# One modulation pair of a delta-rule layer, formed with one-column TensorE products beside the S5 stage

## The reference

```python
c_act = jax.nn.silu(c)
for i in range(DEPTH):
    mod = c_act @ ada_w[i] + ada_b[i]
    sh1, sc1, g1, sh2, sc2, g2 = [m[:, None, :] for m in jnp.split(mod, 6, axis=-1)]
    h = x * (1.0 + sc1) + sh1
    ...
    x = layer_norm(ALPHA * x + (1.0 + g1) * y, ln1_g[i], ln1_b[i])
```

## Time and profile before

| | |
|---|---|
| runs | 2766.16, 2773.31, 2775.39 us; median 2773.31 us |
| the profiled execution | 2767.55 us, its span 2765.9 us |
| TensorE matmul | 2542.9 us busy, 92% of the span |
| VectorE | 2046.9 us, 74% |
| ScalarE | 1220.4 us, 44% |
| chain that ended last | TensorE 74%, VectorE 17%, DMA 3% |
| granted TensorE clock, mean | 0.953 of 2.4 GHz |

### The profile page before, as it was taken

The page is one execution under the profiler, slowest core; times in us unless marked ns, Lnnn a source line. Parts: engine busy times, 40 slices in busy tenths (PEclk is TensorE's granted clock), DMA queues, the critical chain, the costliest instruction groups (busy, mean ns, idle before and its releaser), DMA issues.

```text
span 2765.9 us, 41894 instructions
## 1 busy us (share of the span) xinstructions
PE 2542.9 (92%) x16532; PEld 2298.9 (83%) x16532; DVE 2046.9 (74%) x2518; ACT 1220.4 (44%) x1614; POOL 197.5 (7%) x226
## 2 busy tenths in 40 slices
PE   1499998888889999999999899998999999999998
PEld 1488777777878899889988799998878998899887
DVE  8879999778587777777778888568887655555556
ACT  1255555544455433443343453453464434443444
POOL 0012332000000000000001011000000000000000
PEclk8589999888899999999999899999999999999998
DMA  9874444556448788888888499556588665555652
GB/s 374 285 254 143 152 151 149 195 172 203 138 153 302 272 276 275 277 280 278 277 274 291 154 335 337 173 168 219 183 276 280 214 195 186 190 190 184 196 184 77
DMA packets 272987, 616.02 MB, mean 223 GB/s; under 512 B 23211, under 2 KB 23746, under 8 KB 272578
## 3 DMA queue, kind: packets, MB, share of 16 engines
q1 hardware_dynamic: 240020, 488.00, 52.2%
q0 software_dynamic: 32640, 125.84, 13.0%
q10 hardware_dynamic: 174, 0.04, 0.0%
HBM read 611.73 MB, written 2.10 MB: 222 GB/s over the span
## 4 chain that ended last, share of the span: by engine, by line
PE 74%; DVE 17%; issue 3%; DMA 3%; ACT 2%; SPq 2%; DVEq 0%; POOL 0%; POOLq 0%
PE groups L2530 11%; PE groups L2534 11%; PE groups L2532 11%; PE groups L2538 10%; PE groups L2542 10%; PE groups L2540 10%; DMA ada_units<-in_ada_w_dram 3%; DVE ada_acc L2032 2%; DVE w_lo L2050 2%; SPq L1659 1%; PE pc L2709 1%; DVE ada_acc L872 1%; PE pb L2699 1%; DVE ada_acc L2357 1%; PE groups L1131 1%
## 5 line engine op out<-in xcount | busy, mean ns | idle before, releaser
L1749 ACT ACTIVATE w_hi<-w_raw 128x1024 fp32r<-128x1024 f32 x776 | 817.3, 1059 | 1136.1 <-PE groups L2534 544.6
L2050 DVE TENSOR_TENSOR w_lo<-w_raw,w_hi 128x1024 fp32r<-128x1024 f32 x747 | 905.5, 1223 | 530.4 <-ACT w_hi L1749 526.4
L2530 PE MATMUL groups<-w_hi,act_hi 128*128 128x512 f32 x1408 | 553.4, 393 | 19.8 <-DVE act_lo L2184 19.8
L2534 PE MATMUL groups<-w_lo,act_hi 128*128 128x512 f32 x1408 | 549.9, 391 | 0.0
L2532 PE MATMUL groups<-w_hi,act_lo 128*128 128x512 f32 x1408 | 549.9, 391 | 0.0
L2538 PE MATMUL groups<-act_hi,w_hi 128*128 128x256 f32 x1776 | 511.6, 288 | 33.3 <-DVE act_lo L2184 13.9
L2540 PE MATMUL groups<-act_lo,w_hi 128*128 128x256 f32 x1776 | 503.1, 283 | 0.0
L2542 PE MATMUL groups<-act_hi,w_lo 128*128 128x256 f32 x1776 | 503.0, 283 | 0.0
L2538 PE MATMUL groups<-hid_hi,w_hi 128*128 128x256 f32 x1392 | 390.6, 281 | 0.0
L2542 PE MATMUL groups<-hid_hi,w_lo 128*128 128x256 f32 x1392 | 388.9, 279 | 0.0
L2540 PE MATMUL groups<-hid_lo,w_hi 128*128 128x256 f32 x1392 | 388.9, 279 | 0.0
(11 more groups left out here) (440 smaller groups left out, 2498.6 us busy)
## 6 DMA issues: line engine op xcount, KB each, us to landing
ada_units<-in_ada_w_dram POOLq DMA_DIRECT2D x120, 1024.0 KB, 6.5
w_raw<-in_ffn_w_gate_dram SPq DMA_DIRECT2D x88, 1024.0 KB, 5.2
w_raw<-in_ffn_w_up_dram SPq DMA_DIRECT2D x88, 1024.0 KB, 5.3
w_raw<-in_ffn_w_down_dram SPq DMA_DIRECT2D x88, 1024.0 KB, 5.1
w_raw<-in_cd_w_in_dram SPq DMA_DIRECT2D x48, 1024.0 KB, 5.8
w_raw<-in_ab_w_in_dram SPq DMA_DIRECT2D x40, 1024.0 KB, 5.8
ada_units<-in_ada_w_dram SPq DMA_DIRECT2D x80, 512.0 KB, 4.4
w_raw<-in_ab_w_out_dram SPq DMA_DIRECT2D x16, 1024.0 KB, 6.0
```

Of the source, the lines that this page charges most:

```text
L1749: act.activation(whi[:, half, k], raw[:, slot, k], ACT.Copy).then_inc(hi_done, 1)
L2050: dve.tensor_tensor(wlo[:, half, k], raw[:, slot, k], whi[:, half, k].bitcast(F32), ALU.subtract).then_inc(lo_done, 1)
L2530: pe.matmul(dst, hi[:, k, rows], whi[:, j % 2, kk], start=(k == 0), stop=False, skip_group_check=True)
L2534: last = pe.matmul(dst, hi[:, k, rows], wlo[:, j % 2, kk], start=False, stop=(k == UK * p["units"] - 1), skip_group_check=True)
```

## The change

For the first pair, VectorE's sums go away. TensorE takes each loaded slice as weights and the column of `c_act` that belongs to it as the moving operand: eight products of one column (`ada_columns`), which add up in `pm` over the 16 slices. They stand behind the 48 matmuls of the same 16 units, ahead of `s5_out`. The first pair has no `ada_sum` in the GLU product any more. The semaphore `dn_ada_dve` is called `dn_ada_used`, and TensorE raises it for the first 16 slices; SyncE waits for it at the same places. `take(0)` waits for the count 16 of it.

```diff
--- before.py
+++ after.py
@@ -173,7 +173,7 @@
 
 def pe_names():
 
-    names = [f"ada{b}" for b in range(EARLY_PAIRS)] + ["nq0", "nk0", "gi0", "bi0", "gram0"]
+    names = ["nq0", "nk0", "gi0", "bi0", "gram0"]
     for i in range(ROUNDS):
         nxt = i + 1 < ROUNDS
         early = ["", f"gi{i + 1}", f"bi{i + 1}", "", "", f"nq{i + 1}", ""]
@@ -400,7 +400,7 @@
         dne = Marks(sem("dn_pe"), pe_names())
         dnp = Marks(sem("dn_pool"), pool_names())
         dn_ada_in = [sem(f"dn_ada_in{n}") for n in range(4)]
-        dn_ada_dve = sem("dn_ada_dve")
+        dn_ada_used = sem("dn_ada_used")
         level_masks = sem("dn_level_masks")
         scd = Steps(sem("sc_dve"), "m c0 c1 c2 g", start=1)
         mix_hi, mix_lo = sem("mix_hi"), sem("mix_lo")
@@ -567,7 +567,7 @@
             if m == 0:
                 sp.wait_ge(ada_step, 16 * glu["ab1"] + ADA_FREE)
             if m > 3:
-                sp.wait_ge(dn_ada_dve, m - 3)
+                sp.wait_ge(dn_ada_used, m - 3)
             rows, block = P * (m % 16), glu["ab1"] + 2 * (m // 16)
             sp.dma_start(ada_slot(m), ada_w[0][rows:rows + P, GROUP * block:GROUP * block + 2 * GROUP]
                          ).then_inc(dn_ada_in[m % 4], 16)
@@ -864,17 +864,25 @@
             unit, total = ada_slot(n), ada_total(pair)
             dve.wait_ge(dn_ada_in[n % 4], 16 * (n // 4 + 1))
             if k == 0:
-                if pair > 1:
+                if pair > 2:
                     dve.wait_ge(dne.sem, dne.at(f"ada{pair - 2}"))
                 last = dve.tensor_scalar(total, unit, cact[:, 0:1], None, ALU.mult)
             else:
-                dve.wait_ge(dn_ada_dve, n)
+                dve.wait_ge(dn_ada_used, n)
                 last = dve.scalar_tensor_tensor(total, unit, cact[:, k:k + 1], total, ALU.mult, ALU.add)
-            last.then_inc(dn_ada_dve, 1)
+            last.then_inc(dn_ada_used, 1)
+
+        def ada_columns(pe, m):
+
+            if m == 0:
+                pe.wait_ge(mod_taken, glu["ab1"] + 1)
+            pe.wait_ge(dn_ada_in[m % 4], 16 * (m // 4 + 1))
+            for t in range(2 * GT):
+                last = pe.matmul(pm[:, t:t + 1], ada_slot(m)[:, P * t:P * t + P], cact[:, m:m + 1], start=(m == 0 and t == 0),
+                                 stop=(m == KT - 1), skip_group_check=True)
+            last.then_inc(dn_ada_used, 1)
 
         def deltanet_early_dve(dve, n):
-            if n in EARLY_AT:
-                ada_op(dve, EARLY_AT.index(n))
             if n in CONV_AT:
                 convolve(dve, 0, [CONV_AT.index(n)])
             if n == 30:
@@ -1006,7 +1014,10 @@
                                               ALU.mult, ALU.subtract), f"lo{i}")
 
             def take(pair):
-                on(dne, f"ada{pair}")
+                if pair:
+                    on(dne, f"ada{pair}")
+                else:
+                    dve.wait_ge(dn_ada_used, KT)
                 c = GT * (glu["ab1"] + 2 * pair)
                 done(dve.tensor_tensor(mod[:, c:c + 2 * GT], pm[:, 0:2 * GT], adab[:, c:c + 2 * GT], ALU.add), f"take{pair}")
                 if pair == 0:
@@ -1273,19 +1284,14 @@
                 done(last, f"x{i}.{k}")
 
             def ada_sum(pair):
-                if pair:
-                    on(dnd, f"take{pair - 1}")
-                else:
-                    pe.wait_ge(mod_taken, glu["ab1"] + 1)
-                pe.wait_ge(dn_ada_dve, KT * (pair + 1))
+                on(dnd, f"take{pair - 1}")
+                pe.wait_ge(dn_ada_used, KT * (pair + 1))
                 for t in range(2 * GT):
                     last = pe.matmul(pm[:, t:t + 1], ada_total(pair)[:, P * t:P * t + P], ones[:, 0:1], start=True, stop=True)
                 done(last, f"ada{pair}")
 
             for n in range(4):
                 side(glu, n)
-            for pair in range(EARLY_PAIRS):
-                ada_sum(pair)
             side(glu, 4)
             norm_q(0)
             norm_k(0)
@@ -2711,6 +2717,8 @@
 
             def s5_after(i, j):
                 n = 8 * i + j
+                if n in EARLY_AT:
+                    ada_columns(pe, EARLY_AT.index(n))
                 s5_out(n)
                 if n + 1 < S5_TILES:
                     s5_in(n + 1)
```

## The result

The changed kernel takes 2776.84 us (median of 20 runs, 2768.97 to 2786.40) and the kernel before 2769.62 us (20 runs, 2763.36 to 2775.87). The ratio is 1.0025, with a 95% interval of 1.0016 to 1.0035: a small loss, clear of noise and under the 0.3% up to which the prediction counted a difference as none. The profiled execution is 2773.31 us with a span of 2771.5, 5.6 us over the span before.

A forecast was written before the change was run, and what follows sets the result against it. VectorE was taken to set the S5 stage's pace, with TensorE nearly level. A GLU start 9.4 us later less 3.4 us gained there gave +6, 2773.6 or 2779.3 by base; forecast 2778 us, range 2770 to 2789.

The forecast's parts named there:

- The price of the columns: S5 stage: each unit's 16 one-column records cost TensorE 1.65 us, 26.4 us for 16 units.
- What could be won: S5 stage, units 4 to 31: TensorE's waits, worth 14.8 us at its own period of 8.13 us.
- The start of the GLU product: Behind unit 31: the GLU product starts at 477.5 instead of 468.12, +9.4 us, with some 0.6 us idle ahead.
- The GLU product: First to fifth side: full clock and the removed sum shorten 10.11 us to 6.75, -3.4 us.
- The sum: Whole kernel: +9.4 - 3.4 = +6 us, with column cost bounds +5.5 to +8.4.
- Falling clock in the stage: Rival, S5 stage: the columns stream almost nothing, so TensorE's clock drops; +12 to +24 us, 2785 to 2800; chance 0.14.
- Hidden weight loads: Rival, S5 stage: weight loads hide under the S5 products, 0.4 us a column group, -13 us, 2765; chance 0.03.
- Nothing measurable: Rival, delta rule's rounds: shifting clock falls swallow the 6 us, near 0, 2771 to 2774; chance 0.14.
- Slow start of the GLU product: Rival, GLU product: it starts slow all the same, its gain halves, about +8 us, 2780; chance 0.08.
- waits for slices: Rival, units of the S5 stage: they wait for their slices' loads; chance 0.01.

The follow-up runs named there:

- tail_op: The changed kernel with one more VectorE operation of 128x1024 (result unused) ahead of silu_k in unit 31; 2778.59 us (1 run).
- sum_back: The changed kernel with eight one-column products (results unused) put back between the GLU product's fourth and fifth side; 2768.64 us (1 run).
- fill_full: The kernel before with eight float32 products of 128 columns (16 records) in TensorE's idle time ahead of the GLU product; 2763.87 us (1 run).
- after_again: The changed kernel unedited, timed once more beside 29 runs of the kernel before; 2775.02 us (12 runs), ratio 1.0018 to the kernel before.
- cols_twelve: The changed kernel with four of each slice's eight one-column products issued twice, so groups of 24 records; 2829.57 us (2 runs).
- cols_one: The changed kernel with one one-column product of each slice instead of eight, so groups of 2 records; 2752.88 us (1 run).
- cols_twice: The changed kernel with every one-column product issued twice in a row, so groups of 32 records; 2855.64 us (1 run).
- fill_thin: The kernel before with sixteen one-column float32 products (32 records) in TensorE's idle time ahead of the GLU product; 2762.45 us (1 run).
- cols_fill_two: The changed kernel with two float32 products of 256 columns (results unused) ahead of the one-column products of slices 1 to 15; 2778.41 us (1 run).
- mix_four: The kernel before with only slices 3, 7, 11 and 15 moved to TensorE, three in half groups; 2762.55 us (12 runs), ratio 0.9982.

## Why the prediction was right

- **The price of the columns** was read from the sum that the change removes: 1.65 us a unit forecast, 1.68 measured; 9.8 and 8.1 us between output products, as forecast. The output product of unit 31 was put at 475.5 and came at 475.30.
- **What could be won** were TensorE's waits, 14.8 us by the earlier trace rows and a period of 8.13. They are gone but for three short ones (8.31 or 8.32 in place of 8.13, 0.6 us in all, forecast 0.9). Unit 31's output product came 12.38 us later, which is 16 x 1.68 = 26.9 us of columns less 14.5 of waits.
- **The start of the GLU product**, forecast at 477.5 with 0.6 us of idle time, came at 477.19 with 0.41: +9.07 for +9.4. That the tail is a chain of VectorE's in which the last `ada_op` is worth 1.2 us is shown by tail_op.
- **The GLU product**, forecast at -3.4, gave -3.34, and VectorE's wait for `row_b` was just used up, as foreseen. sum_back and fill_full show how it divides: 2.6 to 2.8 for the clock, some 0.5 for the sum. The prediction did not divide it.
- **The sum**, +6, is 5.73 in the trace at the fifth side; this is the figure that shows the mechanism. That the spans differ by 5.6 as well is luck: from the fifth side to the layer norm behind the rounds it took 278.6 us before and 278.3 in the changed kernel's trace, but 281.6 in after_again. The medians differ by 7.2 in one set and by 4.7 in the other, around the sum. That 2778 is only 1.2 us over the median of 2776.84 is partly luck too: its base (2778 - 6 = 2772) was 2.4 us over the 2769.62 that 20 runs gave, and the difference of the medians was 1.2 over the sum. The bounds given for the sum, +5.5 to +8.4, are +5.4 to +8.3 by its own terms.
- **Rivals.** *Falling clock in the stage*: not in this kernel (four traces at 1.00), but its mechanism is right, and it was nearer than the prediction could see: with eight records more a group it comes, and costs 42 us. The prediction priced it at 12 to 24, by two to six stretches of 3 us each; in cols_twelve the clock is at half for about a quarter of the stage, in stretches of up to 10 us. *Hidden weight loads*: refuted by the group itself (1.68 us), and by cols_one, cols_twelve and cols_twice, which keep 0.111 us a record. *Nothing measurable*: what lies behind the fifth side does shift from one execution to the next (273.4 to 283.3 us from there to the layer norm in fourteen traces), more than the 5.7 us. It has no direction that these traces show: the mean is 278.5 us in the five traces of the kernel before and its variants and 279.0 in the nine of the changed kernel and its variants. So it blurs the 5.7 us and does not eat them, and the interval of the ratio, 1.0016 to 1.0035, leaves zero out. *Slow start of the GLU product* and *waits for slices*: neither shows.

What stays open is how long a group of columns may be before the clock falls: 16 records did not, 24 did, in this stage with its S5 products beside them.

## What to carry to other kernels

Work that moves from the engine that bounds a stage to the one just behind it wins, in that stage, at most the second engine's waits, and is then paid in full; count both before moving, and move only as much as fills the waits. Here four slices of sixteen gave a gain where all sixteen gave a loss. A float32 product of one column cost two records of 0.107 to 0.111 us here, as long as its weight loads, and streams next to nothing, so a run of them can also cost the clock of what stands behind it. Keep the group short: 16 records kept the clock here, 24 did not. Whether streaming products beside 24 records would hold it, no run shows.

## What the hardware showed that was not expected

- **In these runs TensorE's clock went by what streams, and not by how busy it is.** 32 one-column records with no idle time behind them (fill_thin) let it fall from 2.4 to 1.2 GHz; after 16 records of 128 columns and 1.74 us of idle time (fill_full) it stayed. In the stage, groups of 24 records of one column brought it down again and again, and groups of 16 of them with 4 records of 256 columns, in the same time, not once.
- **The first unit of the stage differs from one execution to the next**: from unit 0's output product to unit 1's it took 8.10 us in sum_back and cols_fill_two, 11.26 in the kernel before, 11.62 in the changed one and 12.91 in mix_four and fill_thin. TensorE stands idle for 2 to 5 us ahead of it. The stretch from 194 us on, of the kernel before and of sum_back:

```profile
194.00:204.00 10.00, 10.00 (x54) 8.76 (x52) 8.29 (x11) 5.12 (x9) 3.47 (x3) 0.66 0.33 107
```

```profile
194.00:201.00 7.00, 7.00 (x54) 6.19 (x52) 6.42 (x10) 3.24 (x7) 2.48 (x2) 1.00 0.46 152
```

54 records take 10 us where the clock is down for part of it, and 7 at full clock. That unit is the same in all these kernels, so its extremes are 4.8 us of scatter between executions, nearly as much as the effect studied here, and the reason why stages had to be compared from unit 1 on.
